# A new order of ScalarE's and VectorE's work at the entry of each FFN

## The chip, the cores and the metric

The kernel runs on one core of one Trainium2 chip. The metric is the device time of one execution in microseconds (us). The text uses the engine names of the profile: PE is TensorE, ACT is ScalarE, DVE is VectorE, POOL is GpSimd, SP is SyncE; SPq is SP's DMA queue.

## The reference

One inference step of a backbone with 4 layers and a model width of 1024, on 128 context tokens and 512 latent tokens (640 in all). Each layer is a token mixer and then a gated convolutional FFN, both behind an RMSNorm and a modulation computed from the conditioning vector. Only the FFN matters here:

```python
def conv_ffn(h, w_in, conv_w, conv_b, w_out):
    u = h @ w_in                                   # 1024 -> 2 * 2816
    up = jnp.pad(u, ((0, 0), (1, 1), (0, 0)))
    uc = up[:, :-2] * conv_w[0] + up[:, 1:-1] * conv_w[1] + up[:, 2:] * conv_w[2] + conv_b
    a, b = jnp.split(uc, 2, axis=-1)
    return (jax.nn.silu(a) * b) @ w_out            # 2816 -> 1024
```

Everything is float32. The kernel splits each matmul operand into a high part that TensorE takes as it is and a low part (what the rounding left), and adds three products.

## The kernel before, in words

**Iterations.** The FFN of a layer is cut into 11 iterations of 4 tiles of 128 rows of u: tiles 0 and 2 of a pair p belong to a, tiles 1 and 3 to b (in the code, ft = 0..3, p = ft // 2). Iteration 0 computes its four tiles plainly: first_u_tiles (tiles 0 and 1, into psA) and u_tile(2), u_tile(3) (into psB). From iteration 1 on, each pair of tiles is computed by a scheme with 7 products instead of 8 (product_u, q = 0..6, 12 matmuls each), from sums of halves of h (t_hi, t_lo, computed once per layer) and sums of halves of the weights. out_pass(it) multiplies with w_out, 8 tiles of 12 matmuls, and DVE adds each to xT (out_add).

**The entry.** In each layer PE's order is: first_u_tiles, u_tile(2), u_tile(3), products q0..q6 of (iteration 1, pair 0), out_pass(0), products of (1, pair 1), and so on. What PE waits for in that stretch:

- q0: evac(1) (tiles 0 and 1 copied out of psA) and the low part of weight group 0.
- q2 adds onto the psA bank in which q0's result stands, so it waits for first_part(1,0), ACT's copy of q0 to part_y; also for h_sum_lo(0) and (1) (a count of two) and weight group 2.
- q4: second_part(1,0) and the third h_sum_lo. q5 writes the bank of q3, so it waits for third_part(1,0), the copy to part_z. q6: fourth_part(1,0), the fourth h_sum_lo, weight group 3.
- out_pass(0): in layers 0 to 2 PE first does mod_ffn(l,1,0) (16 matmuls on m_half, a part of the next layer's modulation weights, L2495), for which that 1 MB must have landed. Then it waits for glo(0,1) and for wolo(0,0) and wolo(0,1) (the low parts of w_out). Its tile d from 2 on waits for out_add(0, d-2).

**The other engines** each have one list, executed strictly in the order written. ACT copies results out of PSUM (evac, first_part to fifth_part), begins the convolutions (conv_first), makes high parts (split_product of weights, split_h of the h sums, wohi of w_out, ghi of the gated product) and does silu. DVE makes the sums of h (`H_SUMS`, L3223), ends the convolutions (conv_end), multiplies (gate), makes low parts (product_lo, h_sum_lo, wolo, glo), the weight sums (w_sums) and the additions (add_first, last_half, add_second, out_add). POOL only starts the accumulating loads of weight sums (L2234). In ffn_iter, to_first_half holds the end of the iteration before; for iteration 1 it therefore holds the end of iteration 0's work (evac(3), conv_first(0,3), conv_end(0,2) and (0,3), gate(0,1), glo(0,1) and so on).

**SP's list**, not touched by the change, starts the loads, and each waits for what frees its buffer. At the FFN entry, after the loads of iteration 1, it reads (L2143 on):

```python
next_wo(0)            # waits for s_wolo: wolo(0,0) and wolo(0,1); then 1 MB to wo_stage
load_sums(2, 0)       # 2 x 256 KB
load_first(2, 0)      # 512 KB
load_last(1, 1)       # 256 KB to w_last: the weight sums of (1, pair 1), DVE's w_sums(1,1), take it
if more:              # layers 0 to 2
    used_m_half(l, 0, 1)
    load_m_half(l, 1, 0)   # 1 MB to m_half: mod_ffn(l,1,0), ahead of out_pass(0), takes it
ffn_loads(1)
```

w_sums(1,1) stands in DVE's list directly behind product_lo(1,1,0), and ahead of last_half(1,0), add_second(1,0), conv_end(1,0) and out_add(0,0).

Of the kernel before, what the change touches and what calls it, by code (L numbers as in the profile page):

```python
# [25 lines left out]
ALU = mybir.AluOpType  # L26
# [112 lines left out]
def program(nc, t):  # L139
    with ExitStack() as ctx:  # L140
# [151 lines left out]
        psA = ctx.enter_context(nc.psum_tensor("psA", [P, 4, BANK], F32))  # L292
# [154 lines left out]
        def mod_taken(bank, c=0):  # L447
            return psA[:, bank, c:c + 2 * P].rearrange("p (a n) -> p a n", n=P)

        def mod_pass(l, m):  # L450

            return m + MOD_PASSES * (l + 1)
# [2101 lines left out]
        def _(act):  # L2554
# [53 lines left out]
            for l in range(DEPTH):  # L2608
# [61 lines left out]
                def evac(ft):  # L2670

                    act.wait_ge(s_wused, UNITS * oF + 2 * ft + 2)
                    if ft >= 2:
                        act.wait_ge(s_conv, 4 * ITERS * l + ft - 1)
                    ctx, lat = tokens(psA if ft < 2 else psB, ft % 2)
                    act.activation(u_raw[ft % 2][:, CTX0:CTX0 + SEQ], ctx, ACT.Copy)
                    act.activation(u_raw[ft % 2][:, LAT0:LAT0 + DEC_SEQ], lat, ACT.Copy).then_inc(s_u, 1)
# [6 lines left out]
                def first_part(it, p):  # L2684
                    if not (isinstance(it, int) and (it, p) == (1, 0)):
                        act.wait_ge(s_cv, nth(l, it, p, 2, -1))
                    taken(it, p, 0, part_y[:, :], psA[:, 3 * p, 0:HALF]).then_inc(s_ev, 1)

                def second_part(it, p):
                    act.wait_ge(s_conv, it * 4 + (4 * ITERS * l + 2 * p - 1))  # L2690
                    taken(it, p, 2, u_raw[0][:, SECOND], psA[:, 3 * p, 0:HALF]).then_inc(s_ev, 1)
# [30 lines left out]
                def conv_first(it, ft):  # L2722

                    if not (isinstance(it, int) and it == 0 and ft < 2):
                        act.wait_ge(s_g, it * 2 + (2 * ITERS * l + ft // 2))
                    conv_begin(it, ft, conv[ft % 2])

                def split_product(it, p, g):
                    a, b = GROUPS[g]
                    if isinstance(it, int) and (it, p) == (1, 0):  # L2730
                        act.wait_ge(s_wused, UNITS * oF + b)
                    else:
                        act.wait_ge(s_su, nth(l, it, p, PRODUCTS, GROUP_FREE[g] - PRODUCTS))
                    if g == 2:
                        act.wait_ge(s_ss, nth(l, it, p, 2, 2))
                    else:
                        act.wait_ge((s_pg[p][0], s_pa[p], None, s_pg[p][2])[g], turn(l, it, 16))
                    src, dst = w_source(it, p, g), w_hi[:, a:b, :]
                    act.activation(dst if g < 3 else w_hi[:, a, :], src, ACT.Copy).then_inc(s_shi, 1)  # L2739
# [6 lines left out]
                def split_h(i):  # L2746

                    act.wait_ge(s_tp, H_SUMS * l + (1, 3, 2, 4)[i])
                    if i < 2:
                        act.wait_ge(s_h, KT * (2 * l + 1))  # L2750
                    else:
                        act.wait_ge(s_wused, UNITS * (oF + 1))
                    act.activation(T_HI[i], T_F32[i], ACT.Copy, scale=-1.0 if i == 1 else 1.0).then_inc(s_thi, 1)  # L2753

                def silu(it, p, dst=conv[0]):
                    act.wait_ge(s_conv, it * 4 + (4 * ITERS * l + 2 * p + 1))
                    act.activation(dst[:, 1:COLS - 1], dst[:, 1:COLS - 1], ACT.Silu).then_inc(s_silu, 1)

                def ghi(it, p, src=conv[0], dst=g_hi):
                    act.wait_ge(s_gate, it * 2 + (2 * ITERS * l + p + 1))  # L2760
                    if dst is g_hi_last:
                        act.wait_ge(s_su, 2 * PRODUCTS * (ITERS - 1) * l + 2 * PRODUCTS * (ITERS - 1))
                    elif p == 0 and not (isinstance(it, int) and it == 0):
                        act.wait_ge(s_o, it * KT + KT * ITERS * l)
                    for o, c, w in ((0, CTX0, SEQ), (SEQ, LAT0, DEC_SEQ)):
                        ins = act.activation(dst[:, p, o:o + w], src[:, c:c + w], ACT.Copy)  # L2766
                    ins.then_inc(s_ghi, 1)
# [11 lines left out]
                    act.activation(w_hi[:, u, :], w_stage[:, u, :], ACT.Copy).then_inc(s_whi, 1)  # L2779

                def to_first_half(it, last=False):
                    first = isinstance(it, int) and it == 1
                    if first:
                        evac(3)
                    else:
                        fifth_part(it - 1, 1)
                    conv_first(it - 1, 3)
                    if first:
                        split_h(2)
                    split_product(it, 0, 3)  # L2790
                    first_part(it, 0)
                    silu(it - 1, 1)
                    if first:
                        split_h(3)
                    second_part(it, 0)
                    split_product(it, 1, 0)
                    ghi(it - 1, 1)
                    third_part(it, 0)
                    fourth_part(it, 0)
                    if last:  # L2800
                        split_product(it, 1, 1)
                        split_product(it, 1, 2)
                    conv_first(it, 0)
                    fifth_part(it, 0)
                    conv_first(it, 1)
# [22 lines left out]

                evac(0)
                evac(1)  # L2830
                conv_first(0, 0)
                conv_first(0, 1)
                silu(0, 0)
                split_product(1, 0, 0)
                wohi(0, 0)
                wohi(0, 1)
                split_h(0)
                ghi(0, 0)
                evac(2)
                split_product(1, 0, 1)  # L2840
                conv_first(0, 2)
                split_h(1)
                split_product(1, 0, 2)
                ffn_iter(1)
                with act.Fori(2, ITERS - 1) as it:
                    ffn_iter(it)
# [1 line left out]
                it = ITERS - 1  # L2848
# [28 lines left out]
        def _(dve):  # L2877
# [142 lines left out]
            for l in range(DEPTH):  # L3020
# [63 lines left out]
                def conv_end(it, ft):  # L3084
                    convolve(it, ft, conv[ft % 2])
# [77 lines left out]
                             mod_pass(l, m) + 1)  # L3163

                def to_first_half(it, last=False):
                    first = isinstance(it, int) and it == 1
                    conv_end(it - 1, 2)
                    if first:
                        h_sum_lo(2)
                    conv_end(it - 1, 3)  # L3170
                    gate(it - 1, 1)
                    product_lo(it, 0, 3)
                    if first:
                        h_sum_lo(3)
                    add_first(it, 0)
                    glo(it - 1, 1)
                    product_lo(it, 1, 0)
                    w_sums(it, 1)
                    last_half(it, 0)
                    if first and l == 0:  # L3180
                        mod_bias(1, 0, psA[:, 3, :].rearrange("p (i q j) -> p i j q", i=4, q=4)[:, :, 0:2, :], mod_pass(0, 0) + 1)
                    add_second(it, 0)
                    if last:
                        product_lo(it, 1, 1)
                        product_lo(it, 1, 2)
                    conv_end(it, 0)
# [29 lines left out]

                f11, f12, f21, f22 = (h_f32[:, k, c] for k in (LOW, HIGH) for c in (A, B))
                dve.wait_ge(s_hf, KT * l + KT)
                for i, (out, a, b, op) in enumerate(((f11, f11, f12, ALU.subtract), (f12, f22, f12, ALU.subtract),
                                                     (f22, f22, f11, ALU.add), (f21, f22, f21, ALU.subtract))):  # L3220
                    if i:
                        dve.wait_ge(s_tp, H_SUMS * l + i)
                    dve.tensor_tensor(out, a, b, op).then_inc(s_tp, 1)  # L3223
                conv_end(0, 0)
                conv_end(0, 1)
                gate(0, 0)
                product_lo(1, 0, 0)
                w_sums(1, 0)
                wolo(0, 0)
                wolo(0, 1)  # L3230
                h_sum_lo(0)
                glo(0, 0)
                product_lo(1, 0, 1)
                h_sum_lo(1)
                product_lo(1, 0, 2)
                if l == 0:
                    dve.wait_ge(s_mraw, 2 * MOD_PASSES + 2)
                    for g in range(2):
                        mod_copy_ffn(0, 0, g, mod_taken(3, 2 * P * g))
                ffn_iter(1)  # L3240
                per = 4 + KT + more
                own_before = own.n
# [152 lines left out]
```

## Time and profile before

| | us |
|---|---|
| runs | 3005.13, 3002.28, 3006.21; median 3005.13 |
| the profiled execution, its own time | 3005.12 |
| its span in the profile | 3003.2 |
| busy: PE / DVE / ACT / POOL | 2899.0 / 2333.4 / 1458.0 / 501.7 |
| FFN entries (start of the products q0) | about 128, 919, 1804, 2584 |

All times below are in us from the start of the span. A timeline row gives start, duration, engine, line of kernel.py, the operation with the names of the tiles it writes and reads, how many instructions were merged, and in brackets the idle time before it with what ended it. Instructions of one engine that don't depend on each other overlap by about 0.1 us, so that starts are the better measure of their cost. Names: u_raw and conv are the tiles of the convolution, wo_lo the low part of w_out, t_lo that of the h sums, h_f the sums of h, g_lo that of the gated product.

### The profile page before, as it was taken

The numbers are of one execution on the slowest core, as the hardware profiler recorded it, in microseconds if no ns is written. First come the engines' busy times: TensorE is split into PE (matmuls) and PEld (weight loads), VectorE is DVE, ScalarE is ACT, GpSimd is POOL, SyncE is SP. The second block draws the span as 40 slices with busy tenths as digits, with TensorE's granted clock in tenths as the row PEclk, the third lists the DMA queues.
The fourth block names the chain that finished last, engine by engine and source line by source line (L and its number), as shares of the span: only waits on it lengthen the run. The fifth ranks groups of instructions, "written<-read, shape, count | busy, mean of one in ns | idle before, by whom it ended". The sixth has DMA issues, their size and how long they took to land. (4 is left out here: it accounts for less than half of the span.)

```text
span 3003.2 us, 54111 instructions
## 1 busy us (share of the span) xinstructions
PE 2899.0 (97%) x19576; PEld 2616.5 (87%) x19576; DVE 2333.4 (78%) x4295; ACT 1458.0 (49%) x2810; POOL 501.7 (17%) x472
## 2 busy tenths in 40 slices
PE   8899999999999999999999899999999889999999
PEld 6799999876699999998876698999998669899999
DVE  6888888777758888888647578888887874988887
ACT  3544445436635444544335455544444663654453
POOL 3000000133310000003237410000012331000000
PEclk9999999999999999999999999999999999999999
DMA  8765555210044555632200225665531003344442
GB/s 332 242 171 159 159 159 143 106 60 1 3 143 142 157 159 159 177 128 68 79 33 8 85 75 162 171 171 157 158 138 60 1 1 102 81 119 117 118 125 74
DMA packets 103527, 353.13 MB, mean 118 GB/s; under 512 B 10065, under 2 KB 16465, under 8 KB 79825
## 3 DMA queue, kind: packets, MB, share of 16 engines
q1 hardware_dynamic: 81618, 309.20, 30.5%
q0 software_dynamic: 21760, 41.95, 8.9%
q8 instruction: 93, 1.52, 0.2%
q14 instruction: 56, 0.46, 0.1%
HBM read 346.90 MB, written 4.21 MB: 117 GB/s over the span
## 5 line engine op out<-in xcount | busy, mean ns | idle before, releaser
L3007 DVE SCALAR_TENSOR_TENSOR xT<-psB,mod,xT 128x128 f32<-128x128 f32 x750 | 378.1, 547 | 125.6 <-PE psB L2252 125.0
L2479 PE MATMUL psA<-t_lo,w_hi 128*128 128x320 f32 x1280 | 399.0, 312 | 0.0
L2479 PE MATMUL psA<-h_hi,w_hi 128*128 128x320 f32 x1280 | 398.5, 311 | 0.0
L2479 PE MATMUL psA<-h_hi,w_lo 128*128 128x320 f32 x1280 | 395.4, 309 | 0.0
L2479 PE MATMUL psA<-h_lo,w_hi 128*128 128x320 f32 x1280 | 394.2, 309 | 0.0
L2234 POOL DMA_DIRECT2D w_stage<-weights_dram x80 | 96.5, 1221 | 1499.9 <-DMA w_stage<-weights_dram 1499.9
L3106 DVE TENSOR_TENSOR w_lo<-w_stage,w_hi 128x1024 fp32r<-128x1024 f32 x240 | 292.4, 1220 | 26.3 <-ACT w_hi L2739 25.8
L2252 PE MATMUL psB<-g_hi,wo_hi 128*128 128x320 f32 x1280 | 295.7, 312 | 3.8 <-DVE xT L3007 3.8
L2252 PE MATMUL psB<-g_lo,wo_hi 128*128 128x320 f32 x1280 | 291.4, 308 | 0.0
L2252 PE MATMUL psB<-g_hi,wo_lo 128*128 128x320 f32 x1280 | 291.4, 309 | 0.0
L2739 ACT ACTIVATE w_hi<-w_stage 128x1024 fp32r<-128x1024 f32 x240 | 249.0, 1052 | 35.2 <-PE psA L2479 31.7
L2479 PEld LDWEIGHTS psA<-h_hi,w_hi 128*128 128x128 f32 x1280 | 240.2, 188 | 11.5 <-issue 11.5
L2479 PEld LDWEIGHTS psA<-t_lo,w_hi 128*128 128x128 f32 x1280 | 243.9, 191 | 0.0
L2479 PEld LDWEIGHTS psA<-h_lo,w_hi 128*128 128x128 f32 x1280 | 240.3, 188 | 0.0
L2479 PEld LDWEIGHTS psA<-h_hi,w_lo 128*128 128x128 f32 x1280 | 240.2, 188 | 0.0
L2766 ACT ACTIVATE g_hi<-conv 128x128 fp32r<-128x128 f32 (+1 forms) x160 | 66.0, 461 | 346.5 <-PE psB L2252 346.5
L2719 ACT ACTIVATE conv<-u_raw,vec_sb 128x642 f32<-128x642 f32 x172 | 158.6, 925 | 153.1 <-DVE u_raw L3142 123.2
L2252 PEld LDWEIGHTS psB<-g_hi,wo_hi 128*128 128x128 f32 x1280 | 212.3, 188 | 18.9 <-issue 12.3
L2479 PE MATMUL psA<-t_hi,w_hi 128*128 128x320 f32 x640 | 205.9, 322 | 19.4 <-ACT part_y L2682 19.4
L2252 PEld LDWEIGHTS psB<-g_lo,wo_hi 128*128 128x128 f32 x1280 | 213.9, 188 | 0.0
L2252 PEld LDWEIGHTS psB<-g_hi,wo_lo 128*128 128x128 f32 x1280 | 213.9, 188 | 0.0
L2479 PE MATMUL psA<-t_hi,w_lo 128*128 128x320 f32 x640 | 201.1, 314 | 0.0
(320 smaller groups left out, 6849.8 us busy)
## 6 DMA issues: line engine op xcount, KB each, us to landing
m_half<-w_mod_dram SPq DMA_DIRECT2D x62, 1024.0 KB, 6.0
w_stage<-weights_dram SPq DMA_DIRECT2D x44, 1024.0 KB, 6.5
wo_stage<-w_out_dram SPq DMA_DIRECT2D x44, 1024.0 KB, 4.8
w_stage<-weights_dram SPq DMA_DIRECT2D x82, 512.0 KB, 4.3
w_stage<-weights_dram SPq DMA_DIRECT2D x160, 256.0 KB, 3.2
w_stage<-weights_dram POOLq DMA_DIRECT2D x80, 512.0 KB, 9.0
m_stage<-w_mod_dram SPq DMA_DIRECT2D x24, 1024.0 KB, 8.7
w_last<-weights_dram SPq DMA_DIRECT2D x76, 256.0 KB, 5.8
```

Of the source, the lines that this page charges most:

```text
L2234: pool.dma_start(w_stage[:, 4 * p + 2:4 * p + 4, :], t["weights"][it + cf:it + cf + 1, :, :] .rearrange("a p (u n) -> (a p) u n", n=UNIT)[ ...
L2252: ins = pe.matmul(o, wp, xp[:, a:b], start=first and n == 0, stop=last and n == 2)
L2479: ins = pe.matmul(psA[:, bank, 0:HALF], w[:, SLOT[q], c], x[q][:, k, :], start=(q in (0, 1, 3) and k == 0 and n == 0), stop=(k == 3 and n ...
L2719: act.activation(dst[:, 1:COLS - 1], u_raw[ft % 2][:, 1:COLS - 1], ACT.Identity, bias=vcol(v + 3), scale=vcol(v + 1)).then_inc(s_cb, 1)
L2739: act.activation(dst if g < 3 else w_hi[:, a, :], src, ACT.Copy).then_inc(s_shi, 1)
L2766: ins = act.activation(dst[:, p, o:o + w], src[:, c:c + w], ACT.Copy)
L3007: ins = dve.scalar_tensor_tensor(out=xT[:, d, c:c + w], in0=tokens(ps, slot)[i], scalar=gate[:, d, i:i + 1], in1=xT[:, d, c:c + w], op0=AL ...
L3106: dve.tensor_tensor(w_lo[:, dst, :], w_source(it, p, g), w_hi[:, dst, :].bitcast(F32), ALU.subtract).then_inc(s_slo, 1)
```

## The change

In iteration 0 of each layer ACT and DVE get a new order of the same instructions; PE, POOL and SP keep theirs. On ACT, evac(3) and first_part(1,0) move ahead of conv_first(0,2), and the high parts of the first weights and h sums move up. On DVE, the low parts of the h sums are made in the order 1, 0, 2, 3 with the fourth sum later, and wolo(0,0) and wolo(0,1), before done ahead of h_sum_lo(0), come behind h_sum_lo(3) and glo(0,1); add_first(1,0) comes behind them. What iteration 1's to_first_half held of iteration 0 stands in the entry's own list now.

```diff
--- before.py
+++ after.py
@@ -2779,22 +2779,15 @@
                     act.activation(w_hi[:, u, :], w_stage[:, u, :], ACT.Copy).then_inc(s_whi, 1)
 
                 def to_first_half(it, last=False):
-                    first = isinstance(it, int) and it == 1
-                    if first:
-                        evac(3)
-                    else:
+                    if not (isinstance(it, int) and it == 1):
                         fifth_part(it - 1, 1)
-                    conv_first(it - 1, 3)
-                    if first:
-                        split_h(2)
-                    split_product(it, 0, 3)
-                    first_part(it, 0)
-                    silu(it - 1, 1)
-                    if first:
-                        split_h(3)
-                    second_part(it, 0)
-                    split_product(it, 1, 0)
-                    ghi(it - 1, 1)
+                        conv_first(it - 1, 3)
+                        split_product(it, 0, 3)
+                        first_part(it, 0)
+                        silu(it - 1, 1)
+                        second_part(it, 0)
+                        split_product(it, 1, 0)
+                        ghi(it - 1, 1)
                     third_part(it, 0)
                     fourth_part(it, 0)
                     if last:
@@ -2828,19 +2821,29 @@
 
                 evac(0)
                 evac(1)
+                split_product(1, 0, 0)
                 conv_first(0, 0)
                 conv_first(0, 1)
+                split_h(0)
+                split_h(1)
                 silu(0, 0)
-                split_product(1, 0, 0)
+                split_product(1, 0, 1)
+                split_product(1, 0, 2)
+                ghi(0, 0)
+                evac(2)
                 wohi(0, 0)
                 wohi(0, 1)
-                split_h(0)
-                ghi(0, 0)
-                evac(2)
-                split_product(1, 0, 1)
+                evac(3)
+                first_part(1, 0)
                 conv_first(0, 2)
-                split_h(1)
-                split_product(1, 0, 2)
+                split_h(2)
+                split_product(1, 0, 3)
+                conv_first(0, 3)
+                second_part(1, 0)
+                silu(0, 1)
+                split_h(3)
+                split_product(1, 1, 0)
+                ghi(0, 1)
                 ffn_iter(1)
                 with act.Fori(2, ITERS - 1) as it:
                     ffn_iter(it)
@@ -3163,22 +3166,16 @@
                              mod_pass(l, m) + 1)
 
                 def to_first_half(it, last=False):
-                    first = isinstance(it, int) and it == 1
-                    conv_end(it - 1, 2)
-                    if first:
-                        h_sum_lo(2)
-                    conv_end(it - 1, 3)
-                    gate(it - 1, 1)
-                    product_lo(it, 0, 3)
-                    if first:
-                        h_sum_lo(3)
-                    add_first(it, 0)
-                    glo(it - 1, 1)
+                    if not (isinstance(it, int) and it == 1):
+                        conv_end(it - 1, 2)
+                        conv_end(it - 1, 3)
+                        gate(it - 1, 1)
+                        product_lo(it, 0, 3)
+                        add_first(it, 0)
+                        glo(it - 1, 1)
                     product_lo(it, 1, 0)
                     w_sums(it, 1)
                     last_half(it, 0)
-                    if first and l == 0:
-                        mod_bias(1, 0, psA[:, 3, :].rearrange("p (i q j) -> p i j q", i=4, q=4)[:, :, 0:2, :], mod_pass(0, 0) + 1)
                     add_second(it, 0)
                     if last:
                         product_lo(it, 1, 1)
@@ -3216,27 +3213,42 @@
 
                 f11, f12, f21, f22 = (h_f32[:, k, c] for k in (LOW, HIGH) for c in (A, B))
                 dve.wait_ge(s_hf, KT * l + KT)
-                for i, (out, a, b, op) in enumerate(((f11, f11, f12, ALU.subtract), (f12, f22, f12, ALU.subtract),
-                                                     (f22, f22, f11, ALU.add), (f21, f22, f21, ALU.subtract))):
+                def h_sum(i):
+                    out, a, b, op = ((f11, f11, f12, ALU.subtract), (f12, f22, f12, ALU.subtract),
+                                     (f22, f22, f11, ALU.add), (f21, f22, f21, ALU.subtract))[i]
                     if i:
                         dve.wait_ge(s_tp, H_SUMS * l + i)
                     dve.tensor_tensor(out, a, b, op).then_inc(s_tp, 1)
+
+                for i in range(3):
+                    h_sum(i)
+                product_lo(1, 0, 0)
                 conv_end(0, 0)
                 conv_end(0, 1)
+                w_sums(1, 0)
                 gate(0, 0)
-                product_lo(1, 0, 0)
-                w_sums(1, 0)
-                wolo(0, 0)
-                wolo(0, 1)
+                h_sum(3)
+                h_sum_lo(1)
+                product_lo(1, 0, 1)
+                product_lo(1, 0, 2)
+                glo(0, 0)
                 h_sum_lo(0)
-                glo(0, 0)
-                product_lo(1, 0, 1)
-                h_sum_lo(1)
-                product_lo(1, 0, 2)
+                conv_end(0, 2)
+                h_sum_lo(2)
                 if l == 0:
                     dve.wait_ge(s_mraw, 2 * MOD_PASSES + 2)
                     for g in range(2):
                         mod_copy_ffn(0, 0, g, mod_taken(3, 2 * P * g))
+                conv_end(0, 3)
+                product_lo(1, 0, 3)
+                gate(0, 1)
+                h_sum_lo(3)
+                wolo(0, 0)
+                glo(0, 1)
+                wolo(0, 1)
+                if l == 0:
+                    mod_bias(1, 0, psA[:, 3, :].rearrange("p (i q j) -> p i j q", i=4, q=4)[:, :, 0:2, :], mod_pass(0, 0) + 1)
+                add_first(1, 0)
                 ffn_iter(1)
                 per = 4 + KT + more
                 own_before = own.n
```

## Rows read from the trace of the kernel before

**Rows 1.** The page, busy time of each engine over the span.

```profile
PE 2899.0 (97%) x19576; PEld 2616.5 (87%) x19576; DVE 2333.4 (78%) x4295; ACT 1458.0 (49%) x2810; POOL 501.7 (17%) x472
```

**Rows 2.** Waits of PE: engine, line, releaser: us in total, times, longest us.

```profile
PE psA L2479 <- ACT part_y L2682: 19.4, 4, 5.5
```

**Rows 3.** Timeline of PE, entries of layers 0 and 1: start us, us, instruction.

```profile
127.69 0.42 PE L2479 MATMUL psA<-h_hi,w_hi 128*128 128x320 f32 x1
...
927.92 0.63 PE L2479 MATMUL psA<-t_hi,w_hi 128*128 128x320 f32 x1 [5.46 <-ACT part_y L2682]
```

**Rows 4.** Windows behind the four stalls; columns: engines, granted clock, DMA share, GB/s.

```profile
134.50:141.30 6.80, 6.75 (x28) 6.74 (x29) 6.66 (x9) 4.15 (x7) 0.00 (x0) 0.54 0.96 292
927.90:934.00 6.10, 6.08 (x27) 6.08 (x28) 5.96 (x8) 4.01 (x7) 0.00 (x0) 0.61 0.94 300
1813.00:1820.00 7.00, 6.43 (x34) 6.43 (x35) 6.86 (x10) 4.74 (x9) 0.16 (x1) 0.76 0.93 286
2593.00:2600.00 7.00, 6.75 (x30) 6.75 (x31) 6.86 (x11) 4.54 (x8) 0.00 (x0) 0.62 0.89 200
```

**Rows 5.** Timeline of VectorE, entry of layer 1.

```profile
916.59 2.35 DVE L3151 TENSOR_TENSOR wo_lo<-wo_stage,wo_hi 128x1024 fp32r<-128x1024 f32 x2
...
923.38 1.49 DVE L3124 SCALAR_TENSOR_TENSOR t_lo<-h_f,t_hi 128x1280 fp32r<-128x1280 f32 x1 [1.09 <-ACT t_hi L2753]
...
933.70 0.55 DVE L3135 TENSOR_TENSOR u_raw<-psA,part_y 128x128 f32<-128x128 f32 x2
934.17 0.89 DVE L3099 TENSOR_TENSOR g_lo<-conv,g_hi 128x128 fp32r<-128x128 f32 x2
```

**Rows 6.** Timeline of VectorE, entries of layers 0, 2 and 3.

```profile
110.27 6.07 DVE L3223 TENSOR_TENSOR h_f<-h_f 128x1280 f32<-128x1280 f32 x4
...
141.46 0.89 DVE L3099 TENSOR_TENSOR g_lo<-conv,g_hi 128x128 fp32r<-128x128 f32 x2
...
1819.82 0.89 DVE L3099 TENSOR_TENSOR g_lo<-conv,g_hi 128x128 fp32r<-128x128 f32 x2
...
2599.51 0.89 DVE L3099 TENSOR_TENSOR g_lo<-conv,g_hi 128x128 fp32r<-128x128 f32 x2
...
2601.56 0.69 DVE L3115 TENSOR_TENSOR w_stage<-w_stage,w_last 128x512 f32<-128x512 f32 x1
...
2606.57 1.01 DVE L3007 SCALAR_TENSOR_TENSOR xT<-psB,mod,xT 128x128 f32<-128x128 f32 x2
```

**Rows 7.** Timeline of SP's DMA issues, entry of layer 1.

```profile
918.97 0.33 SPq L1991 DMA_DIRECT2D wo_stage<-w_out_dram  x1
922.31 4.05 SPq L2086 DMA_DIRECT2D w_stage<-weights_dram  x3
...
926.88 0.43 SPq L2006 DMA_DIRECT2D m_half<-w_mod_dram  x1
```

**Rows 8.** DMA issues near 133.5, 919.0, 926.9 and 1812.5: KB, us to landing.

```profile
m_half<-w_mod_dram SPq DMA_DIRECT2D x1, 1024.0 KB, 9.6
...
wo_stage<-w_out_dram SPq DMA_DIRECT2D x1, 1024.0 KB, 5.5
...
m_half<-w_mod_dram SPq DMA_DIRECT2D x1, 1024.0 KB, 8.2
...
m_half<-w_mod_dram SPq DMA_DIRECT2D x1, 1024.0 KB, 8.7
```

**Rows 9.** A window of layer 1 while w_out loads; columns as in rows 4.

```profile
922.00:923.00 1.00, 0.46 (x4) 0.19 (x2) 0.28 (x1) 1.00 (x2) 0.00 (x0) 1.00 1.02 434
```

**Rows 10.** PE timeline: mod_ffn (layers 0 to 2), layer 3's first out_pass matmuls.

```profile
146.76 1.07 PE L2268 MATMUL psA<-m_half,cond 128*32 128x256 f32 x16
...
939.03 1.07 PE L2268 MATMUL psA<-m_half,cond 128*32 128x256 f32 x16
...
1823.96 1.07 PE L2268 MATMUL psA<-m_half,cond 128*32 128x256 f32 x16
...
2604.44 0.46 PE L2252 MATMUL psB<-g_hi,wo_hi 128*128 128x320 f32 x2
```

## The prediction

> **What bounds the kernel now.** The page comes first: TensorE (PE) is busy 97% of the span [rows 1], so the time moves only where PE's idle time or its clock moves. The waits of PE come next. The largest is that of the FFN products for ScalarE's copy of part_y, four times and 19.4 us in all, once in each layer's FFN entry [rows 2]. The timeline gives its place: in layer 1 q0 and q1 are done at 922.4, and q2 starts only at 927.92, after 5.46 us [rows 3]. 
>
> **Part 1, ScalarE.** The same instructions in another order. first_part(1,0) now stands behind evac(3), and evac(3) behind little. u_tile(3) ends when q0 begins, evac(3) fills the time of q0, and the copy follows q0 directly. q2 then starts without a wait if its low parts are there: VectorE's list puts h_sum_lo(1), slot groups 1 and 2, glo(0,0) and h_sum_lo(0) ahead, and adding up durations and waits along both lists gives 922.1 for the last of them in layer 1 (an estimate), against q1's end at 922.4. The 5.5 us go. What is late next on this engine is third_part(1,0), which empties psA bank 2 for q5. It now stands behind ghi(0,1), which waits for gate(0,1). The same adding up puts gate's end at 928.2, and after 0.8 and 0.4 us of ScalarE the bank is free at 929.4, against q4's end at 927.6: a new stall of about 2 us.
>
> **Part 2, VectorE.** Again the same instructions, but wolo(0,1), before done at 916.59 + 2.35 = 918.94 [rows 5], is now the last but add_first(1,0) (in layer 0 also mod_bias). VectorE's work up to that point is all it did before up to the end of glo(0,1), at 934.17 + 0.89 = 935.06, less add_first (0.47 us of issue, 933.70 to 934.17) and less its one wait of 1.09 us: **933.5** in layer 1 [rows 5]. The other layers by the same subtraction of 1.56: layer 2 from 1820.71 to 1819.15; layer 3 from 2600.40 to 2598.84 [rows 6]. Layer 0 needs one correction: q0 starts at 127.69 there [rows 3], so copy and convolution start let conv_end(0,2) begin no earlier than 130.9, while VectorE, begun at 110.27 [rows 6] with some 18.7 us of listed work ahead of it, is there at 129.0. That adds 1.9: 142.35 - 1.56 + 1.9 = 142.7.
>
> **What hangs on wolo: SP's queue.** No SP line changes, and this decides. next_wo(0) waits for wolo(0,1) before it loads the next w_out, and behind it, in order, stand both load_sums(2,0), load_first(2,0), load_last(1,1) and, in layers 0 to 2, load_m_half(l,1,0). Before, the w_out load left at 918.97, 0.03 us after wolo, and the rest by 926.88 [rows 7]. Now all five or six leave together from 933.5 (0.4 us each). Two of them are needed at once: m_half by mod_ffn, which PE does ahead of out_pass(0), and w_last by VectorE's w_sums(1,1), ahead of everything that leads to out_add(0,0).
>
> How long from wolo to the landing of m_half? Alone, w_out (1 MB) lands after 5.5 us [rows 8]. While it moved, the rate reached 434 GB/s [rows 9]; with the accumulating load beside them the transfers ran at 286 to 300 (last column of rows 4, first three). I take 385 for loads without that company: 2.7 us of the 5.5 are transfer and 2.8 are start and completion, and the 0.5 MB of load_sums add 1.4 us. The remaining 1.75 MB took, with the POOL queue's accumulating load beside them, from about 926.0 (third w_stage issue, 922.31 + 4.05 less its 0.4 [rows 7]) to 926.88 + 8.2 = 935.1, 9.1 us [rows 7, 8]; less the 2.8 us that now overlap, 6.3. So **13.2 us** in layer 1; layer 2 took 0.5 more (8.7) and layer 0 took 1.4 more (9.6) [rows 8]: 13.7 and 14.6. Bounds: 11.0 where the accumulating load costs nothing; 15 to 16 where it takes its full share of the transfers. w_last stands 1 MB earlier: 5.5 + 1.4 + 2.6 (0.75 MB at some 300 GB/s) = 9.5 us, between 8.5 and 11.
>
> The Trainium skill ("DMA: Bandwidth & Descriptors", Specifications and Anatomy of one DMA) gives one core about 358 GB/s from HBM and 2 us fixed. As an estimate by that page, 3.4 MB take 11.5 us, and the sum below would be about 8 us less.
>
> **The sum.** PE's mod_ffn started at 146.76, 939.03 and 1823.96, layer 3's out_pass at 2604.44 [rows 10].
> - Layer 0: 142.7 + 14.6 = 157.3, later by 10.6.
> - Layer 1: 933.5 + 13.2 = 946.7, later by 7.7.
> - Layer 2: 1819.15 + 13.7 = 1832.9, later by 8.9.
> - Layer 3 has no m_half. w_last lands at 2598.84 + 9.5 = 2608.3. From w_sums(1,1) at 2601.56 to the end of out_add(0,0) at 2606.57 + 0.92 it took 5.9 us [rows 6], so out_add(0,0) ends at 2614.3. The third tile of out_pass waits for it; before, that tile began two tiles of 12 matmuls, 3.5 us, behind 2604.44, at 2608.0. Later by 6.3.
>
> Together 33.5. These starts already contain the old clock loss, and PE now idles 10 to 14 us just ahead of them (the 2 us at q5 vanish in that). I expect the same fall of the clock behind each, as after stalls of 4.9 us on average before: 9 us again, bounds 5 (four times the weakest fall) and 13 (four times the strongest). Sum 33.5 + 9 = 42.5. The profiled execution took 3005.12 us with a span of 3003.2, level with the median 3005.13; 3005.1 + 42.5 = **3048**. In the stages behind, PE is the bound as before, and the loads that are late there have 10 us and more of cover.
>
> The Trainium skill ("TensorE: Matmul & The Clock Gate", Part 1) says that activity is judged in windows that run free of the kernel. The spread 0.54 to 0.76 [rows 4] agrees; it would move the clock term within its bounds, not the sign.
>
> **Rivals.**
> 1. The loads are not late: SP's wait does not hold the burst, or the burst lands before PE asks. Then PE loses 5.5 us of stall per entry, gets 2 back at q5 and 2 to 3 at the third tile of out_pass, where VectorE is now late with w_sums, last_half and conv_end; adding up each layer gives 1.3, 3.5, 2.8 and 2.5 us gained, 10 in all, with the clock unchanged: **2995**, faster. It decides in favour if m_half leaves SP before about 933 - 9 = 924 in layer 1; the code's order and wolo's end at 933.5 speak against it, nothing in the trace speaks for it. 3%.
> 2. The gain and the lateness cancel, as with transfers at nearly twice the pace: within 0.2% (6 us, about what a measurement of this kernel can tell from no change). 1%.
> 3. The transfers are quick (11 us) and the clock falls weakly: 33.5 - 10 + 5 = 28.5, **3033 to 3034**. 20%, within slower.
> 4. The lateness spreads: the next m_half and w_last (2,0) leave SP only after PE's mod_ffn and could be late for the end of out_pass. Before, m_half had some 14 us of cover there and took 7 to 9, so another 2 to 5 us per layer at worst: **3060**. 8%.
>
> **Numbers.** The forecast's own case has 68%. Range: lower end 3005 + 33.5 - 10 + 3 = 3031, upper end 3005 + 33.5 + 7 (longer landings) + 13 = 3059. Slower by over 0.2%: 96%; within: 1%; faster: 3%.
>
> **What would show it.** In the changed profile: the wait of q2 for part_y is gone or under 1 us; q5 waits about 2 us for part_z; the w_out load issues near 933 (layer 1), with five or six loads 0.4 us apart; PE's longest waits in each entry are for m_half (DMA), 10 to 14 us, and in layer 3 for xT (VectorE), with VectorE itself waiting for w_last; low clock behind them. It is wrong if the w_out load issues before 924 or mod_ffn starts within 2 us of the old times; the size is wrong if the landing from wolo is not 11 to 16 us.

## The result and the profile after

| | before | after |
|---|---|---|
| median of 4 runs, us | 3005.67 (3002.28 to 3007.54) | 3039.81 (3036.41 to 3045.02) |
| ratio of the two | | 1.0111, 95% interval 1.0097 to 1.0126 |
| span of the profiled execution, us | 3003.2 | 3040.2 |

The change makes the kernel slower by 34 us. PE's longest waits of the changed kernel, where [rows 2] had one line of 19.4 us for part_y (engine, tile, line, releaser: us in total, times, longest us; L2252 is the matmul of out_pass, L2268 that of mod_ffn):

```profile
PE psA L2268 <- DMA m_half<-w_mod_dram: 28.5, 3, 9.9
PE psB L2252 <- DVE xT L3010: 17.1, 13, 9.6
...
PE psA L2479 <- ACT part_z L2682: 7.3, 4, 1.8
```

The wait for part_y at q2 is gone. In its place stand m_half in three layers, xT (13 times, but 9.6 us of it in one, in layer 3), and part_z at q5. VectorE's wait that is new:

```profile
DVE w_stage L3118 <- DMA w_last<-weights_dram: 29.5, 4, 7.5
```

It has four pieces, one in each entry. SP's queue in layer 1 shows where they come from, against [rows 7]:

```profile
941.13 0.33 SPq L1991 DMA_DIRECT2D wo_stage<-w_out_dram  x1
941.50 1.63 SPq L2086 DMA_DIRECT2D w_stage<-weights_dram  x3
943.18 0.44 SPq L2086 DMA_DIRECT2D w_last<-weights_dram  x1
943.66 0.43 SPq L2006 DMA_DIRECT2D m_half<-w_mod_dram  x1
```

Before, w_out left at 918.97 and m_half at 926.88, with w_out, sums, first and last spread over 8 us. Now everything leaves within 3 us of 941.13. That moment is VectorE's last wo_lo, in the timeline against [rows 5]:

```profile
939.88 1.22 DVE L3154 TENSOR_TENSOR wo_lo<-wo_stage,wo_hi 128x1024 fp32r<-128x1024 f32 x1
...
950.12 0.69 DVE L3118 TENSOR_TENSOR w_stage<-w_stage,w_last 128x512 f32<-128x512 f32 x1 [7.42 <-DMA w_last<-weights_dram]
...
957.96 1.01 DVE L3010 SCALAR_TENSOR_TENSOR xT<-psB,mod,xT 128x128 f32<-128x128 f32 x2 [2.76 <-PE psB L2252]
```

wolo(0,1) starts at 939.88 and ends at 941.10, SP issues 0.03 us later, and VectorE itself, after add_first and product_lo(1,1,0), waits 7.42 us for w_last. PE in the same entry, and in layers 0, 2 and 3, against [rows 10]:

```profile
153.85 1.93 PE L2268 MATMUL psA<-m_half,cond 128*32 128x256 f32 x16 [9.93 <-DMA m_half<-w_mod_dram]
...
937.86 0.52 PE L2479 MATMUL psA<-h_hi,w_hi 128*128 128x320 f32 x1 [1.81 <-ACT part_z L2682]
...
952.49 1.93 PE L2268 MATMUL psA<-m_half,cond 128*32 128x256 f32 x16 [9.31 <-DMA m_half<-w_mod_dram]
...
1849.19 1.94 PE L2268 MATMUL psA<-m_half,cond 128*32 128x256 f32 x16 [9.30 <-DMA m_half<-w_mod_dram]
...
2642.24 0.90 PE L2252 MATMUL psB<-g_hi,wo_hi 128*128 128x320 f32 x2 [9.56 <-DVE xT L3010]
```

q5 waits 1.81 us, mod_ffn 9.31 us. m_half lands 11.3 us after the w_out load was issued (943.66 + 8.8 - 941.13):

```profile
m_half<-w_mod_dram SPq DMA_DIRECT2D x1, 1024.0 KB, 8.8
```

Behind the long waits the clock is low, as it was behind the old ones [rows 4]:

```profile
153.85:160.85 7.00, 7.00 (x38) 5.79 (x39) 3.30 (x5) 4.96 (x9) 0.00 (x0) 0.58 0.81 213
952.49:959.49 7.00, 7.00 (x38) 5.72 (x39) 3.30 (x5) 5.48 (x9) 0.00 (x0) 0.57 0.86 227
1849.19:1856.19 7.00, 7.00 (x46) 5.73 (x47) 4.08 (x7) 5.46 (x9) 0.00 (x0) 0.74 0.87 225
2637.00:2650.00 13.00, 7.76 (x35) 7.76 (x36) 9.36 (x16) 5.27 (x8) 0.00 (x0) 0.61 0.22 38
138.60:143.90 5.30, 5.28 (x24) 5.04 (x24) 5.12 (x10) 0.29 (x1) 0.00 (x0) 0.68 0.17 34
```

The missing clock in the first three windows is 2.9 + 3.0 + 1.8 us. The fourth window also holds the end of the stall in layer 3; from PE's restart at 2642.24 to 2650 the granted clock is 0.62 over 7.76 us, another 2.9. Together 10.7, against 9.9 before. The fifth window is new: behind the 1.81 us at q5 the clock falls as well, but what q5 and q6 lose there is covered by the wait for m_half.

**A measure of the entry alone.** Whole runs of one kernel spread by some 5 to 11 us. The entry can be timed in a trace by itself: from evac(0)'s first activation to the first product behind out_pass(0). In layer 1, before and after:

```profile
904.60 0.28 ACT L2676 ACTIVATE u_raw<-psA 128x128 f32<-128x128 f32 x1 [1.38 <-PE psA L2454]
...
955.31 0.41 PE L2479 MATMUL psA<-h_hi,w_hi 128*128 128x320 f32 x1
```

```profile
912.83 0.28 ACT L2676 ACTIVATE u_raw<-psA 128x128 f32<-128x128 f32 x1 [1.39 <-PE psA L2454]
...
971.50 0.41 PE L2479 MATMUL psA<-h_hi,w_hi 128*128 128x320 f32 x1
```

955.31 - 904.60 = 50.7 us before, 971.50 - 912.83 = 58.7 after. The four layers before give 51.8 + 50.7 + 50.0 + 48.6 = 201.1, after 62.2 + 58.7 + 57.6 + 56.7 = 235.1: **34.1 us more, as much as the difference of the medians (34.1)**. The spans of the two traces differ by 37.0, so 2.9 us lie outside the entries; that is within the spread of whole runs, and nothing shows a cause for it. The experiments are given with this sum too; it comes from one trace of each.

### The profile page after: what moved, and what is told of

Its sections match the earlier page's. It is cut to its first block, busy times and chain, and to the rows that moved or that the text cites. A ratio compares the mean times of both kernels' runs of the same rounds, so it can differ in the third digit from the quotient of the medians.

```text
span 3040.2 us, 54111 instructions
## 1 busy us (share of the span) xinstructions
PE 2909.5 (96%) x19576; PEld 2621.8 (86%) x19576; DVE 2331.8 (77%) x4295; ACT 1457.1 (48%) x2810; POOL 501.6 (16%) x472
## 4 chain that ended last, share of the span: by engine, by line
PE 81%; DVE 10%; DMA 3%; ACT 3%; issue 2%; SPq 0%; POOL 0%; DVEq 0%; ACTq 0%
PE psA L2479 29%; PE psB L2252 25%; PE psA L2362 4%; PE psA L2363 4%; PE psA L2368 4%; PE psA L2268 2%; PE psB L838 2%; PE psA L915 2%; DMA w_stage<-weights_dram 1%; DVE top L1754 1%; DVE xs L2972 1%; DMA m_half<-w_mod_dram 1%; PE psB L820 1%; DVE w_lo L3109 1%; PE psB L973 1%
## 5 line engine op out<-in xcount | busy, mean ns | idle before, releaser
L2252 PE MATMUL psB<-g_hi,wo_hi 128*128 128x320 f32 x1280 | 299.0, 315 | 13.4 <-DVE xT L3010 13.4
L2252 PE MATMUL psB<-g_lo,wo_hi 128*128 128x320 f32 x1280 | 293.8, 311 | 0.0
L2252 PE MATMUL psB<-g_hi,wo_lo 128*128 128x320 f32 x1280 | 293.3, 310 | 0.0
L2252 PEld LDWEIGHTS psB<-g_hi,wo_hi 128*128 128x128 f32 x1280 | 215.1, 190 | 29.9 <-DVE xT L3010 16.3
L2252 PEld LDWEIGHTS psB<-g_lo,wo_hi 128*128 128x128 f32 x1280 | 216.8, 190 | 0.0
L2252 PEld LDWEIGHTS psB<-g_hi,wo_lo 128*128 128x128 f32 x1280 | 216.1, 190 | 0.0
```

The lines of the kernel that those rows point to most:

```text
L2252: ins = pe.matmul(o, wp, xp[:, a:b], start=first and n == 0, stop=last and n == 2)
```

## The experiments

The theory: the time of wolo(0,1) is the time of SP's next_wo(0), and so of every load behind it; PE and VectorE wait for those. The rivals: the new order makes VectorE's or ScalarE's own results too late; or w_last, through w_sums and out_add, holds PE in every layer.

| | us, median | ratio, 95% interval | four entries, us |
|---|---|---|---|
| the change | 3039.8 | 1.0111 (1.0097 to 1.0126) | 235.1 |
| e1, SP's list reordered | 3002.2 | 0.9991 (0.9979 to 1.0003) | 194.6 |
| e2, before with wolo late | 3047.5 | 1.0142 (1.0125 to 1.0159) | 241.0 |
| e3, before with e1's edit | 3008.5 | 1.0009 (1.0000 to 1.0019) | 200.6 |
| e4, w_last alone ahead | 3032.8 | 1.0092 (1.0075 to 1.0108) | 225.9 |
| e5, e1 and part_z early | 3009.2 | 1.0008 (0.9999 to 1.0017) | 200.7 |
| e6, e5 and w_sums late | 3006.1 | 1.0003 (0.9994 to 1.0012) | 199.5 |
| e7, the change with wolo earlier | 2998.7 | 0.9977 (0.9967 to 0.9986) | 192.4 |
| e8, e1 and e7 together | 2998.3 | 0.9976 (0.9967 to 0.9985) | 193.8 |
| e9, before with the copy early | 3007.0 | 1.0003 (0.9993 to 1.0012) | 201.9 |

The ratios are to the kernel before on the same chip (medians 3005.7 to 3006.1).

Every run also has its mean granted clock on record. The share that is missing, times the span, averaged over the runs of a kernel, tells how much of a difference the clock made. It is an estimate: the clock is recorded to 0.001, which is 3 us in a single run, and a low clock costs nothing while PE waits. For the experiments that end near the kernel before (before on the same chip in brackets, 19 to 27 runs; 10 to 12 of each experiment):

| | clock missing, us | mean span less that, us |
|---|---|---|
| e1 | 18.3 (23.6) | 2982.9 (2980.4) |
| e5 | 23.2 (23.7) | 2982.7 (2980.4) |
| e6 | 16.1 (23.7) | 2988.3 (2980.4) |
| e7 | 16.8 (23.7) | 2980.4 (2980.4) |
| e8 | 17.1 (23.2) | 2979.6 (2980.7) |
| e9 | 23.0 (23.2) | 2982.1 (2980.7) |

**e1. The change, and SP no longer held by wolo.**

```diff
-                next_wo(0)
                 load_sums(2, 0)
                 load_first(2, 0)
                 load_last(1, 1)
                 if more:
                     used_m_half(l, 0, 1)
                     load_m_half(l, 1, 0)
+                next_wo(0)
                 ffn_loads(1)
```

> The changed kernel with one edit on SP: next_wo(0) stands behind load_sums(2,0), load_first(2,0), load_last(1,1) and load_m_half(l,1,0) instead of ahead of them. Theory (the loads held up behind next_wo are the cost): w_last and m_half issue near 920 in layer 1, PE's waits for m_half (28.5 us) and VectorE's for w_last (29.5 us) go, and of the gain of the first copy a part shows: 3001 us, between 2994 and 3007. What stays is the wait of q5 for part_z (7.3 us in all) and one of 2 to 3 us per entry for out_add(0,0). Rival (the new order of VectorE and ScalarE is itself too late for out_pass): 3025 us or more.

3002.2 us: 37.6 us come back by one line moved on an engine that the change never touched. SP in layer 1:

```profile
917.19 1.46 SPq L2086 DMA_DIRECT2D w_stage<-weights_dram  x3
918.69 0.43 SPq L2086 DMA_DIRECT2D w_last<-weights_dram  x1
919.17 0.43 SPq L2006 DMA_DIRECT2D m_half<-w_mod_dram  x1
931.19 0.33 SPq L1991 DMA_DIRECT2D wo_stage<-w_out_dram  x1
```

The needed loads leave 12 us ahead of w_out, whose own lateness shows in no wait of PE. PE's waits:

```profile
PE psB L2252 <- DVE xT L3010: 15.7, 16, 3.6
...
PE psA L2479 <- ACT part_z L2682: 7.3, 4, 1.8
```

part_z stays with 7.3 us, m_half is gone, and xT is 15.7 in all, with 3.6 in layer 3. The rival that asked for 3025 falls. Against before the gain is not clear of zero in the runs (0.9979 to 1.0003). The entries are 6.4 us shorter in the trace, and the table above puts the gain to the clock (18.3 us missing against 23.6), not to the waits.

**e2. The kernel before, and wolo late.**

```diff
-                wolo(0, 0)
-                wolo(0, 1)
                 h_sum_lo(0)
...
                     glo(it - 1, 1)
+                    if first:
+                        wolo(0, 0)
+                        wolo(0, 1)
```

> The kernel before with one edit on VectorE: wolo(0,0) and wolo(0,1) stand behind glo(0,1), everything else in the old order. Theory: the burst of loads issues near 936.5 in layer 1, m_half lands 11.3 us later, PE's wait for m_half is 8 to 9 us in layers 0 to 2 and as much for xT in layer 3; with the old stall of q2 kept and a second fall of the clock: 3050 us, between 3040 and 3058. Rival (the cost of the change lies in the other moves): within 10 us of before.

3047.5 us, slower than the change. This one move is enough for the whole loss, and the rest of the change softens it:

```profile
PE psA L2268 <- DMA m_half<-w_mod_dram: 34.5, 3, 12.0
PE psB L2252 <- DVE xT L3007: 18.6, 13, 10.9
...
PE psA L2479 <- ACT part_y L2682: 10.3, 4, 3.2
```

12.0 us at most for m_half in one layer, 10.9 for xT in layer 3. Of part_y's 19.4 us, 10.3 are left. ScalarE's conv_first(0,2) stands ahead of the copy to part_y and waits for VectorE's glo(0,0); without wolo ahead of it, glo(0,0) comes sooner. Layer 1, in the kernel before and in e2:

```profile
921.18 0.93 ACT L2719 ACTIVATE conv<-u_raw,vec_sb 128x642 f32<-128x642 f32 x1 [2.66 <-DVE g_lo L3099]
```

```profile
926.41 0.93 ACT L2719 ACTIVATE conv<-u_raw,vec_sb 128x642 f32<-128x642 f32 x1 [0.39 <-DVE g_lo L3099]
```

This wait is 2.27 us shorter and q2's is 2.29 us shorter (3.17 in place of 5.46). So the old wait for part_y was in part wolo's own doing.

**e3. The kernel before, and e1's edit.** The edit is that of e1.

> The kernel before with the edit on SP of e1 alone. The w_out load moves behind loads that were not late. Both theories: no difference, 3005 us within 3.

3008.5 us, 0.5 above the 3 us that were allowed, but 1.0009 (1.0000 to 1.0019) of before, and the entries are 200.6 against 201.1. The edit gains nothing where wolo is early, so e1's 37.6 us are what was held up, not a better order of loads as such.

**e4. The change, and only w_last freed.**

```diff
+                load_last(1, 1)
                 next_wo(0)
                 load_sums(2, 0)
                 load_first(2, 0)
-                load_last(1, 1)
```

> The changed kernel with load_last(1,1) alone moved ahead of next_wo(0) on SP. Theory (m_half holds PE in layers 0 to 2, w_last in layer 3 only): VectorE's waits for w_last go in all four layers, layer 3 loses its stall of 9.6 us and the low clock behind it, layers 0 to 2 keep theirs: 3031 us, between 3026 and 3035. Rival (w_last, through w_sums and out_add, holds PE in all layers): 3005 or less.

3032.8. By layers the entries are 61.0, 58.3, 57.5 and 49.0 against 62.2, 58.7, 57.6 and 56.7 of the change: 7.7 us off in layer 3, and 1.2, 0.3 and 0 in the others. VectorE's wait for w_last is gone in all four, PE's for m_half is not:

```profile
PE psA L2268 <- DMA m_half<-w_mod_dram: 29.9, 3, 10.5
...
PE psB L2252 <- DVE xT L3010: 10.9, 13, 3.6
```

So m_half holds PE in layers 0 to 2 and w_last in layer 3 only, as foretold; the rival that put it all on w_last falls.

**e5. e1, and part_z ahead of ghi(0,1).**

```diff
                 split_product(1, 1, 0)
-                ghi(0, 1)
...
                     third_part(it, 0)
+                    if isinstance(it, int) and it == 1:
+                        ghi(0, 1)
                     fourth_part(it, 0)
```

> e1 with one more edit on ScalarE: ghi(0,1) behind third_part(1,0) instead of ahead of it. Theory (behind the loads, VectorE's way to out_add(0,0) is the next bound): the wait of q5 for part_z, 7.3 us in all, goes, and the wait of out_pass for xT grows by about as much; within 3 us of e1's 3002. Rival (each wait of PE costs its own length): 2994 or less.

The wait for part_z (7.3 us) is gone and out_pass waits 6.1 us more for xT (21.8 us against 15.7):

```profile
PE psB L2252 <- DVE xT L3011: 21.8, 16, 3.8
```

That is the theory's exchange of waits, but the result was expected within 3 us of e1 and is 7 above it: 200.7 us in the entries against 194.6. The clock explains it. One stall of 2.9 to 3.8 us stands where e1 had one of 1.8 and one of 0.9 to 3.6, and behind all four of them it falls (windows of 7 us from PE's restart, layers 1, 2, 3 and 0):

```profile
939.30:946.30 7.00, 6.97 (x38) 6.97 (x39) 5.31 (x10) 2.20 (x4) 0.00 (x0) 0.79 0.00 1
1824.70:1831.70 7.00, 6.99 (x32) 6.99 (x33) 5.12 (x9) 1.89 (x4) 0.00 (x0) 0.64 0.02 5
2605.90:2612.90 7.00, 6.94 (x30) 6.95 (x31) 4.93 (x10) 1.67 (x3) 0.00 (x0) 0.61 0.01 2
149.90:156.90 7.00, 6.96 (x37) 6.97 (x38) 5.25 (x9) 1.92 (x4) 0.00 (x0) 0.76 0.01 2
```

1.5 + 2.5 + 2.7 + 1.7 = 8.4 us of clock are missing. e1 has three falls, behind q5 in layers 0 and 2 and behind the third tile in layer 3, and in layer 1 none (windows of 7 us in layers 1, 2, 3 and 0):

```profile
938.80:945.80 7.00, 6.94 (x47) 6.95 (x48) 6.45 (x13) 2.22 (x4) 0.00 (x0) 1.00 0.02 7
1815.50:1822.50 7.00, 7.00 (x48) 6.23 (x48) 5.88 (x10) 1.39 (x4) 0.00 (x0) 0.79 0.64 220
2602.30:2609.30 7.00, 6.98 (x37) 6.99 (x38) 5.23 (x9) 1.63 (x3) 0.00 (x0) 0.76 0.01 2
138.30:145.30 7.00, 6.98 (x45) 6.21 (x46) 6.90 (x14) 0.30 (x1) 0.00 (x0) 0.76 0.40 132
```

0 + 1.5 + 1.7 + 1.7 = 4.9 us. In these traces that is 3.5 of the 6.1 us between the entries. Over all runs, whose means differ by 4.8 us, it is the whole difference: 4.9 us more clock is missing in e5, and the rest of the span is level (2982.7 and 2982.9). So the exchange of waits was about even, and the lower clock made e5 slower.

**e6. e5, and VectorE's product_lo(1,1,0) and w_sums(1,1) behind out_add(0,1).**

```diff
-                    product_lo(it, 1, 0)
-                    w_sums(it, 1)
+                    if not (isinstance(it, int) and it == 1):
+                        product_lo(it, 1, 0)
+                        w_sums(it, 1)
                     last_half(it, 0)
...
                     out_add(it - 1, 1)
                     conv_right(it, 1, conv[1], step)
+                    if isinstance(it, int) and it == 1:
+                        product_lo(it, 1, 0)
+                        w_sums(it, 1)
```

> e5 with one more edit on VectorE: product_lo(1,1,0) and w_sums(1,1), some 2.5 us together, stand behind out_add(0,1) and the convolution's end instead of ahead of last_half(1,0). Theory: out_add(0,0) ends 2.5 us earlier in each of the four entries and with it out_pass: 10 us below e5, 2991, between 2985 and 2997. Rival (something else holds the third tile of out_pass): as e5, about 3001.

A miss: 3006.1, not 2991. The third tile does start 2.6 us sooner after mod_ffn (6.2 us behind it in layer 1, against 8.7 in e5), but what was moved is only paid at a later tile. The waits of PE in layer 1, in order of time:

```profile
936.12 0.56 PE L2252 MATMUL psB<-g_hi,wo_hi 128*128 128x320 f32 x2 [1.25 <-DVE xT L3011]
...
942.13 0.56 PE L2252 MATMUL psB<-g_hi,wo_hi 128*128 128x320 f32 x2 [2.23 <-DVE xT L3011]
...
945.57 0.56 PE L2252 MATMUL psB<-g_hi,wo_hi 128*128 128x320 f32 x2 [1.41 <-DVE xT L3011]
```

1.25 + 2.23 + 1.41 = 4.9 us in three pieces, against 3.8 in one. VectorE is full from the h sums into the middle of out_pass; moving its work within that stretch moves the wait, it does not remove it. The median hides part of this: over the runs e6 has 7.1 us less clock missing than e5 and the rest of its span is 5.6 us longer. So the clock stayed higher behind the shorter stalls, and the move itself cost time; where that time goes beyond the waits for xT (24.9 us against 21.8) no run shows.

**e7. The change, SP as it was, and wolo behind h_sum_lo(0).**

```diff
                 glo(0, 0)
                 h_sum_lo(0)
+                wolo(0, 0)
+                wolo(0, 1)
                 conv_end(0, 2)
...
                 h_sum_lo(3)
-                wolo(0, 0)
                 glo(0, 1)
-                wolo(0, 1)
```

> The changed kernel, SP's list untouched, with wolo(0,0) and wolo(0,1) moved up to stand behind h_sum_lo(0), ahead of conv_end(0,2). Theory (the time of wolo(0,1) sets everything through SP's queue): the w_out load issues 8.4 us earlier than in the changed kernel, m_half lands at about the time PE asks, its wait of 28.5 us shrinks to under 5 and the low clock behind it with it: 3005 us, between 2999 and 3011. Rival (it is not the place of wolo that counts but the order of the rest): 3030 or more.

2998.7 us, 0.3 below the lower end: **faster than both kernels**, 0.9977 (0.9967 to 0.9986). Here the w_out load leaves 8.4 us sooner after evac(0) than in the change, and m_half is waited for twice, 2.2 us in all. New is a wait of 1.6 us at q4 in layers 1 to 3. The profile names no releaser for it ("issue"); q4 needs h_sum_lo(2), which is late by the 2.3 us of wolo and ends 0.1 us before q4 starts (923.48 and 923.58 in layer 1):

```profile
PE psA L2479 <- ACT part_z L2682: 8.4, 4, 2.2
...
PE psA L2479 <- issue: 4.9, 3, 1.6
...
PE psA L2268 <- DMA m_half<-w_mod_dram: 2.2, 2, 1.7
```

The gain over the kernel before is nearly all clock: 16.8 us missing against 23.7 over the runs, with the rest of the span level at 2980.4. Before, each entry had one long stall (3.1 us in layer 0, 5.5 in the others), and the clock fell behind all four. e7 has stalls of 1.6 to 2.2 us in their place.

**e8. e1 and e7 together.** Both edits, as above.

> The changed kernel with both edits: wolo(0,0) and wolo(0,1) behind h_sum_lo(0) (e7) and next_wo(0) behind the other loads on SP (e1). Theory: what e7 still waits for m_half (0.5 us in layer 1, 1.7 in layer 2) goes, no more: 2997 us, between 2993 and 3001. Rival (the loads still cost more than their waits show): 2993 or less.

2998.3, 0.9976 (0.9967 to 0.9985): level with e7. The last 2.2 us of m_half's wait are gone from the trace and too small to show in the runs. The gain over before is again the clock's for the most part (17.1 us missing against 23.2, the rest 1.1 us shorter).

**e9. The kernel before, and the first copy early.**

```diff
                 split_product(1, 0, 1)
+                evac(3)
+                first_part(1, 0)
                 conv_first(0, 2)
```

(and the two calls taken out of iteration 1's to_first_half)

> The kernel before with one edit on ScalarE: evac(3) and first_part(1,0) stand ahead of conv_first(0,2); VectorE and SP as before, so wolo stays early. Theory (the copy early gains by itself, until the next late step): q2 waits for VectorE's third product_lo, which ends near 926.0 in layer 1, so its wait shrinks by 1.5 to 2 us per layer and no load is late: 2999 us, between 2996 and 3003. Rival (the copy is hidden behind the same VectorE work anyway): 3005.

A miss of 8 us: no gain, 1.0003 (0.9993 to 1.0012). The first half of the expectation holds, q2 waits for VectorE's w_lo now and 14.6 us in place of 19.4:

```profile
PE psA L2479 <- DVE w_lo L3107: 14.6, 4, 3.7
...
PE psB L2252 <- DVE xT L3008: 10.2, 14, 2.6
```

Those 4.8 us come back behind it: 2.6 more for xT (10.2 against 7.6), and in layer 0 waits of 1.0 us for part_z and 1.6 for the modulation ahead of mod_ffn. The copy alone is worth nothing without VectorE's new order; and the two together are worth something only where wolo does not hold up the loads (e7 and e8; in e1 the gain is not clear of zero).

## Why the prediction was right

**The sign and the mechanism** were right at each step: q2's wait gone; q5 waiting about 2 us for part_z (1.8); the w_out load at wolo's end; m_half holding PE in layers 0 to 2 and w_last, through w_sums and out_add(0,0), in layer 3; a fall of the clock behind each of these waits. e1, e2 and e4 show the cause by taking it away, by making it alone, and by freeing one of the two loads.

**The size** was 42.5 us against 34.1, inside the range. The terms, each from evac(0) on, since the stretch ahead of the entries moved by a few us:

| | predicted | measured |
|---|---|---|
| layer 0, mod_ffn later by | 10.6 | 7.7 |
| layer 1 | 7.7 | 5.2 |
| layer 2 | 8.9 | 6.0 |
| layer 3, third tile later by | 6.3 | 5.4 |
| clock | 9 | 9.8 |

The clock's 9.8 is what the stretch from these starts to the end of the entry grew by (2.7, 2.7, 1.6 and 2.8 us); the windows behind the waits give 10.7. So the measured terms make 34.1 by the way they are taken, and the sum is no check of its own. The mis-sized term is the landing of m_half after wolo: I took 13.2, 13.7 and 14.6 us, and it was 11.3, 11.3 and 11.8. I had carried over the full company of the POOL queue's accumulating load from the old schedule and taken 5.5 us for w_out. The accumulating load was not there: before, in layer 1, POOL started it 0.5 us ahead of m_half (926.33), and its queue moved 0.39 of the 2.23 MB while m_half was under way; after, it started only at 948.45, and it was 0.02 of 3.24 MB. And the 5.5 us for w_out was the slowest of the four entries before (4.8, 5.5, 4.7 and 4.6); in the burst it took 4.7 to 5.0. The measured 11.3 is nearly the lower bound (11.0). The rest of the gap is VectorE's list, where wolo(0,1) ended 0.3 to 0.6 us sooner than counted, which no run takes apart further, and in layer 3 w_last, which was there for VectorE after 9.1 us and not 9.5.

The measured 11.3 is also close to the 11.5 us estimated from the Trainium skill ("DMA: Bandwidth & Descriptors", Specifications and Anatomy of one DMA), by which the sum would have been 34.5 us. The two agree in the total only. The Trainium skill gives its 2 us in that section for the path of DMAs started by GpSimd, and its 358 GB/s as one core's half of what the memory gives. The loads here were started by SP, and this trace moved 434 GB/s from 943 to 944 us; no run takes the two terms apart.

**Sums of the prediction that do not come out.** The lower bound of 11.0 for the landing: at its own 385 GB/s, 5.5 + 1.4 + 4.8 make 11.7, so the measured 11.3 is quicker than its case without company. The lower bound of the clock, four times the weakest fall, is 6.7 and not 5 (and the range took 3). Neither moves the forecast.

**Rival 1** (2995, the loads not late) describes what e1 and e7 do once the loads are early: 3002.2 and 2998.7. Its 10 us of gain with the clock unchanged were too many, and its own terms don't give them: 5.5 less 2 at q5, less 2 to 3 at the third tile, is 0.5 to 1.5 per entry, and less in layer 0, where the stall was 3.1. In e1 the waits for part_y, part_z and xT together fell from 27.0 to 23.0 us, and the clock did change, in e1's favour (4.9 us missing against 9.9). **Rival 4** (lateness spreading) did not happen: PE waits for m_half three times and VectorE for w_last four times in the whole trace, each time inside an entry.

## What to carry to other kernels

Before work is moved to a later place in one engine's list, look up every semaphore it raises and every queue that waits on one of them. wolo looked free: before, it was done 21 us ahead of out_pass(0), the first to need its result, and the change moved it back by 14. But it also freed a buffer, and SP, which runs its list in order, had five other loads (in layers 0 to 2) behind that wait. Put a load that waits for something late behind the loads that don't. And where one engine is full over a whole stretch, a wait removed early in it comes back later in it (e5, e6, e9): measure the stretch, not the wait. Last, look at the clock before a gain of some us is put to a wait: what e7 gained and what e5 lost against e1 were the clock's.

## What the runs showed of the hardware

The clock does not follow the length of a stall alone. In the changed kernel it fell behind stalls of 1.84 and 1.81 us at q5 (0.68 over the 5.3 us behind the first, above; 0.67 over 5.1 us behind the second). In e1 PE stalled at q5 for 1.81 or 1.82 us in each of the four entries; over 7 us behind them the granted clock was 0.76, 1.00, 0.79 and 1.00. In e9 PE stood 3.57 us ahead of q2 in layer 0, and the clock stayed full:

```profile
133.88 0.39 PE L2479 MATMUL psA<-t_hi,w_hi 128*128 128x320 f32 x1 [3.57 <-DVE w_lo L3107]
```

```profile
130.00:145.00 15.00, 10.12 (x67) 9.30 (x65) 13.69 (x18) 9.09 (x13) 1.20 (x1) 1.00 0.67 195
```

Behind its stalls of 3.67 to 3.69 us in layers 1 to 3 it was 0.56, 0.76 and 0.76 over 7 us. So the clock term of one stall can't be read from its length; over the four entries of one trace it came out at 9.9 us before and 10.7 after. The Trainium skill ("TensorE: Matmul & The Clock Gate", Part 1) has the activity judged in windows that run free of the kernel. Unequal clocks behind equal stalls agree with that; no run here shows the windows themselves.

The clock is also most of the spread between runs of one kernel. Of 27 runs of the kernel before on one chip, the longest (3011.53 us) had a mean granted clock of 0.989, the shortest (3000.18 us) 0.994.

And a burst of seven loads (3.5 MB with the second w_last) behind one wait landed hardly slower than the spread loads did: in layer 1 m_half took 8.8 us from its own issue, against 8.2 before. At its issue five loads of SP's queue had not landed, where before there were two. But before, the accumulating load ran beside it, and after it hardly did (0.02 MB); while m_half was under way the core moved 368 GB/s, against 272 before. No run separates the two.
